# One step of a hybrid decoder: gating stage in another order, unit matrix first, residual loads in SyncE's queue

## What is computed

```python
# layer 0, part B: chunked gating
vn = layer_norm(v, ln_g, ln_b)
ws = tril(w_s)                                   # 8 groups of 128x128
mixed = einsum('gij,bcjgd->bcigd', ws, vp) + b_s # vp: vn in chunks
out_b = u * mixed * silu(gate)
# layer 0, sample group: 8 queries over 256 cached keys (2 pages each) and their own
p = softmax(logits + alibi + mask); o = p @ v_sel
x1 = LayerNorm(ALPHA * x + concat(out_a, out_b) @ e_w_out)
# layer 1: recurrence over time, per head, with S of 64x64
S = S * w_t + sa * (kk_t * a_t) + v_t * k_t;  out_t = S @ r_t
y = LayerNorm(ALPHA * x1 + gated(out) @ c_w_out)
```

## Time and profile before

| | us |
|---|---|
| median of 3 runs | 2238.67 (2236.12 to 2243.87) |
| profiled execution | 2245.97 |
| its span, first to last instruction | 2244.2 |
| PE busy | 1830.0 (82%) |
| DVE busy | 1239.5 (55%) |
| ACT busy | 575.7 |
| POOL busy | 402.2 |
| gating stage | 879 to 1113 |
| recurrence | 1806 to 2048 |
| last projection | 2051 to 2244 |

### The profile page before, as it was taken

How to read it: one execution, slowest core, us unless ns; L and a number is a source line. 1 busy time by engine, 2 the same in 40 slices (tenths; PEclk the granted TensorE clock), 3 DMA queues, 4 the chain that set the end, 5 groups by cost and what they waited for, 6 DMA issues and landing times. The chain is left out here.

```text
span 2244.2 us, 30621 instructions
## 1 busy us (share of the span) xinstructions
PE 1830.0 (82%) x11638; PEld 1063.9 (47%) x11638; DVE 1239.5 (55%) x2382; ACT 575.7 (26%) x1153; POOL 402.2 (18%) x376
## 2 busy tenths in 40 slices
PE   8999467899984996599747999978989947772877
PEld 4445134444433774365233666644455436662432
DVE  2000074888897763654466667677533326562485
ACT  0000015400013552111045545561122014340100
POOL 0001110000023552110000233320013312232110
PEclk9999688999996998689876999988988979995999
DMA  4100724222111003621164344534847395755510
GB/s 176 71 33 34 208 73 129 80 75 72 75 39 67 29 20 116 220 99 44 59 129 170 104 140 139 146 116 101 146 124 137 95 218 140 183 135 162 171 67 38
DMA packets 277601, 245.65 MB, mean 109 GB/s; under 512 B 131997, under 2 KB 229309, under 8 KB 277197
## 3 DMA queue, kind: packets, MB, share of 16 engines
q1 hardware_dynamic: 271988, 227.36, 35.7%
q0 software_dynamic: 2976, 9.02, 1.1%
q10 hardware_dynamic: 2496, 7.37, 1.1%
HBM read 161.60 MB, written 86.63 MB: 111 GB/s over the span
## 5 line engine op out<-in xcount | busy, mean ns | idle before, releaser
L1761 PE MATMUL ri_ps<-ri_xm,ri_w 128*128 128x384 f32 (+1 forms) x768 | 233.1, 458 | 0.1
L555 PE MATMUL ix_ps<-ix_src,ei_xT 128*128 128x512 f32 x512 | 223.5, 599 | 9.3 <-DMA ix_src<-in_e_w_in 9.3
L1857 PE MATMUL ri_ps<-ri_w,ri_xm 128*128 128x512 f32 x512 | 227.3, 607 | 0.0
L186 PE MATMUL ei_ps<-ei_w,ei_xT 128*128 128x512 f32 (+1 forms) x432 | 188.4, 598 | 3.9 <-DMA ei_w<-in_e_w_in 3.9
L1761 PEld LDWEIGHTS ri_ps<-ri_xm,ri_w 128*128 128x128 f32 x768 | 145.2, 191 | 73.8 <-issue 2.6
L633 DVE TENSOR_SCALAR_CACHE_REDUCE ix_flags<-score,ix_cand 128x384 bf16<-128x384 f32 (+1 forms) x186 | 163.7, 943 | 12.2 <-DVE ix_cand L650 12.0
L555 PEld LDWEIGHTS ix_ps<-ix_src,ei_xT 128*128 128x128 f32 x512 | 98.0, 192 | 132.3 <-issue 122.8
L1857 PEld LDWEIGHTS ri_ps<-ri_w,ri_xm 128*128 128x128 f32 x512 | 99.6, 195 | 124.8 <-issue 124.7
L1348 PE MATMUL co_psm<-co_w,co_srcT 128*128 128x512 f32 (+1 forms) x288 | 128.6, 606 | 15.2 <-DVE co_y L1403 14.4
L186 PEld LDWEIGHTS ei_ps<-ei_w,ei_xT 128*128 128x128 f32 (+1 forms) x432 | 77.6, 181 | 113.8 <-issue 113.8
L1106 PE MATMUL go_psm<-go_w,go_srcT 128*128 128x512 f32 (+1 forms) x288 | 129.7, 610 | 0.0
(11 more groups left out here) (328 smaller groups left out, 3021.6 us busy)
## 6 DMA issues: line engine op xcount, KB each, us to landing
ix_src<-in_e_w_in SPq DMA_DIRECT2D x4, 2048.0 KB, 11.1
scratch_h<-ix_stage SPq DMA_DIRECT2D x32, 256.0 KB
ri_w<-in_c_w_in SPq DMA_DIRECT2D x16, 512.0 KB, 5.6
ri_w<-in_c_w_in SPq DMA_DIRECT2D x4, 2048.0 KB, 8.6
ei_w<-in_e_w_in SPq DMA_DIRECT2D x3, 2048.0 KB, 19.6
scratch_h<-ei_stage POOLq DMA_DIRECT2D x24, 256.0 KB, 2.3
ix_src<-scratch_h SPq DMA_DIRECT2D x3, 2048.0 KB, 8.4
go_uvg<-scratch_h SPq DMA_DIRECT2D x8, 768.0 KB, 6.6
```

What stands on the lines that cost most here:

```text
L186: last = nc.tensor.matmul(ps[n % NB][0:rows(t), 0:cw], xT[:, kd, t * P:t * P + rows(t)], rhs, start=(kd == 0), stop=(kd == KD - 1))
L555: last = nc.tensor.matmul(ps[n % NB][:], xT[:, kd, t * P:(t + 1) * P], w_rest[s % 2][:, kd], start=(kd == 0), stop=(kd == KD - 1))
L1761: last = nc.tensor.matmul(out[:, 0:wd], w[:, ct % 2, kd, i * P:(i + 1) * P], xm[:, i, kd, lo:lo + wd], start=(kd == 0), stop=(kd == KD - 1))
L1857: last = nc.tensor.matmul(out[:], xm[:, j, kd, t * P:(t + 1) * P], w[:, a, kd], start=(kd == 0), stop=(kd == KD - 1))
```

## The change

1. Gating stage, SyncE: `upper` is issued ahead of uvg(0); w(0) goes ahead of src(0) and uvg(1); uvg(2) and src(1) go ahead of the sample's loads; the loads of `w00` and `b00` go to the end of the prologue and get a semaphore of their own, waited for only by the last tile's gate. The 16 page loads are issued in four parts, in steps 1 to 4, behind load_uvg.
2. Gating stage, TensorE: a step is project(s-2), mixed(s), transposes(s-1). `turn` is in step 5, and the value products come in steps 6 and 7, four samples in each.
3. Gating stage, ScalarE and VectorE: the y activation (L1154) stands ahead of the srcT copies. The sample's softmax stands behind `finish`, its first half in step 2, its second in step 3, `shares` in step 4 and `own_value` in step 5.
4. Recurrence: the two loads of `eye` go first in the queue.
5. Last projection: all residual, gain and offset loads leave ScalarE's queue for SyncE's. res(0), gain and offset stand behind src(2), the sample step's whole part 0 (`side.sync(sp, 0)`) behind them, then src(3), res(1), src(4), res(2) and so on.

```diff
-    def pages(self, sp):
-        sp.wait_ge(self.pt_in, 16)
+    def pages(self, sp, part):
+        if part == 0:
+            sp.wait_ge(self.pt_in, 16)
...
-        for b in range(DB):
+        for b in (2 * part, 2 * part + 1):
...
@@ phase_gate_out, SyncE
+            sp.dma_start(upper[:], g["c_uppereq"]).then_inc(c_in, 16)
             load_uvg(0)
-            sp.dma_start(upper[:], g["c_uppereq"]).then_inc(c_in, 16)
             sp.dma_start(bgam[:], ...).then_inc(c_in, 16)
             sp.dma_start(bbet[:], ...).then_inc(c_in, 16)
             sp.dma_start(bs[:], ...).then_inc(c_in, 16)
+            load_w(0)
             load_src(0)
             load_uvg(1)
-            load_w(0)
             load_w(1)
-            sp.dma_start(w00[:], ...).then_inc(c_in, 16)
-            sp.dma_start(b00[:], ...).then_inc(c_in, 16)
+            load_uvg(2)
+            load_src(1)
             side.loads(sp)
-            load_src(1)
             load_res(0)
...
-            load_uvg(2)
             load_src(2)
             load_res(1)
-            side.pages(sp)
             load_res(2)
+            sp.dma_start(w00[:], ...).then_inc(own_in, 16)
+            sp.dma_start(b00[:], ...).then_inc(own_in, 16)
             for s in range(1, NT + 4):
                 if s + 2 <= LAST:
                     load_uvg(s + 2)
+                if s <= 4:
+                    side.pages(sp, s - 1)
@@ phase_gate_out, TensorE
             for s in range(NT + 3):
+                if s >= 2:
+                    project(s - 2)
                 if s < NT:
                     mixed(s)
-                if s == 3:
+                if s == 5:
                     side.turn(pe)
-                if 4 <= s < 4 + DB // 2:
-                    side.values(pe, 2 * (s - 4))
+                if s in (6, 7):
+                    side.values(pe, 4 * (s - 6))
...
                     transposes(s - 1)
-                if s >= 2:
-                    project(s - 2)
@@ phase_gate_out, VectorE
-            dve.wait_ge(c_in, 16 * 6)
+            dve.wait_ge(c_in, 16 * 4)
...
                     gate(s - 1)
-                if s == 1:
-                    side.logits(dve)
-                if s == 2:
-                    side.shares(dve)
-                if s == 4:
-                    side.own_value(dve)
...
                 if s >= 3:
                     finish(s - 3)
+                if s in (2, 3):
+                    side.logits(dve, s - 2)
+                if s == 4:
+                    side.shares(dve)
+                if s == 5:
+                    side.own_value(dve)
@@ phase_out, SyncE
             for t in tiles:
+                if t == 3:
+                    side.sync(sp, 0)
                 if t not in side.late:
                     load_src(sp, t)
...
+                else:
+                    load_res(t - 2)
+                if t == 2:
+                    sp.dma_start(gam[:], gain_d.partition_broadcast(P)).then_inc(g_in, 16)
+                    sp.dma_start(bet[:], bias_d.partition_broadcast(P)).then_inc(g_in, 16)
+            for t in (NT - 1, NT):
+                load_res(t)
@@ phase_wkv, SyncE
+            for h in range(2):
+                sp.dma_start(eye[half(h)], g["c_ident"][half(h), half(h)]).then_inc(c_in, 16)
             load_bk(0)
             load_ra(0)
             sp.dma_start(mb[:], g["c_mb"]).then_inc(c_in, 16)
-            for h in range(2):
-                sp.dma_start(eye[half(h)], g["c_ident"][half(h), half(h)]).then_inc(c_in, 16)
```

More of the change, by code:

```diff
@@ L886, in scalar, with logits @@
         self.nc.scalar.activation(self.lrow[:], self.lrow[:], ACT.Exp).then_inc(self.exped, 1)
-    def logits(self, dve):
+    def logits(self, dve, part):
         nc, lrow, mx = self.nc, self.lrow, self.mx
-        self.link = link = Chain(dve, self.link_v)
-        dve.wait_ge(self.own_in, 16 * 3)
-        link(nc.vector.tensor_tensor(lrow[:], lrow[:], self.alibi[:], ALU.add))
-        link(nc.vector.tensor_tensor(lrow[:], lrow[:], self.score_s[0:DB, 0:SKEYS].unsqueeze(1).broadcast_to([DB, H, SKEYS]), ALU.add))
+        if part == 0:
+            self.link = Chain(dve, self.link_v)
+        link = self.link
+        if part == 0:
+            dve.wait_ge(self.own_in, 16 * 3)
+            link(nc.vector.tensor_tensor(lrow[:], lrow[:], self.alibi[:], ALU.add))
+            link(nc.vector.tensor_tensor(lrow[:], lrow[:], self.score_s[0:DB, 0:SKEYS].unsqueeze(1).broadcast_to([DB, H, SKEYS]), ALU.add))
+            return
         link(nc.vector.tensor_reduce(mx[:], lrow[:], AX.X, ALU.max))
@@ L935, in values @@
         pe.wait_ge(self.cache_in, 16 * 2 * DB)
-        for b in range(b0, b0 + 2):
+        for b in range(b0, b0 + DB // 2):
             for ct in range(4):
@@ L984, in phase_gate_out @@
         uvg_in, src_in, res_in = ([sem(f"{n}{i}") for i in range(RING)] for n in ("uvg_in", "src_in", "res_in"))
-        ws_tr, wsT_d, half_d = sem("ws_tr"), sem("wsT_d"), sem("half_d")
+        ws_tr, wsT_d, half_d, own_in = sem("ws_tr"), sem("wsT_d"), sem("half_d"), sem("own_in")
         boff_d, bnorm_d, off_d, norm_d = sem("boff_d"), sem("bnorm_d"), sem("off_d"), sem("norm_d")
@@ L1043, in _ @@
             sp.dma_start(bet[:], g["ln_b"][0].partition_broadcast(P)).then_inc(g_in, 16)
-            load_uvg(2)
             load_src(2)
             load_res(1)
-            side.pages(sp)
             load_res(2)
+            sp.dma_start(w00[:], g["b_ws"][:, 0, 0:1].rearrange("g o -> (g o)").partition_broadcast(DB), **small).then_inc(own_in, 16)
+            sp.dma_start(b00[:], g["b_bs"][:, 0:1].rearrange("g o -> (g o)").partition_broadcast(DB), **small).then_inc(own_in, 16)
             for s in range(1, NT + 4):
@@ L1138, in _ @@
                     nc.scalar.activation(vn[0:m, k], slot(uvg, s)[:, AW:2 * AW], ACT.Identity, scale=brs[0:m, k:k + 1], bias=boff[0:m, k:k + 1]).then_inc(bnorm_d, 1)
-                if s == 2:
+                if s >= 3:
+                    t = s - 3
+                    m, k = rows(t), t % 2
+                    act.wait_ge(off_d, t + 1)
+                    nc.scalar.activation(y[0:m, k], y[0:m, k], ACT.Identity, scale=rstd[0:m, k:k + 1], bias=off[0:m, k:k + 1]).then_inc(norm_d, 1)
+                if s == 4:
                     side.scalar(act)
@@ L1149, in _ @@
                                        ps_t[half][:].rearrange("p (j n) -> p j n", j=4)[:, :, 0:m]).then_inc(srcT_d, 1)
-                if s >= 3:
-                    t = s - 3
-                    m, k = rows(t), t % 2
-                    act.wait_ge(off_d, t + 1)
-                    nc.scalar.activation(y[0:m, k], y[0:m, k], ACT.Identity, scale=rstd[0:m, k:k + 1], bias=off[0:m, k:k + 1]).then_inc(norm_d, 1)
         @block.gpsimd
@@ L1204, in gate @@
                     dve.wait_ge(vn_d, t + 1)
+                    dve.wait_ge(own_in, 32)
                     link(nc.vector.tensor_tensor(hd(o), hd(vn[0:m, k]), w00[:].unsqueeze(2).broadcast_to([DB, H, HD]), ALU.mult))
@@ L1294, in _, with load_res @@
         def _(sp):
+            def load_res(t):
+                sp.dma_start(res[0:rows(t), t], residual_of(t)).then_inc(res_in[t], 16)
             sp.dma_start(ident[:], ident_d).then_inc(c_in, 16)
             for t in tiles:
+                if t == 3:
+                    side.sync(sp, 0)
                 if t not in side.late:
                     load_src(sp, t)
-                if t == 0:
-                    side.loads(sp)
                 if t < 2:
@@ L1353, in _ @@
         def _(act):
-            for t in tiles:
-                act.dma_start(res[0:rows(t), t], residual_of(t)).then_inc(res_in[t], 16)
-                if t == 1:
-                    act.dma_start(gam[:], gain_d.partition_broadcast(P)).then_inc(g_in, 16)
-                    act.dma_start(bet[:], bias_d.partition_broadcast(P)).then_inc(g_in, 16)
             for n in range(2 * (NT + 1)):
```

9 lines of the change are left out of this document (4 added, 5 removed).

## The result

| | before | after |
|---|---|---|
| median of 4 runs, us | 2241.27 (2236.12 to 2248.51) | 2211.15 (2206.20 to 2214.73) |
| profiled execution, span | 2244.2 | 2211.4 |
| mean granted TensorE clock | 0.889 | 0.897 |

The ratio is 0.9864, 95% interval 0.9844 to 0.9884: 30 us faster. 2207 was forecast, 2193 to 2222 the range.

A forecast was written before the change was run, and what follows sets the result against it. No one engine bounds the kernel; five stages follow each other with barriers, three touched. Gains of 16.7 (28.8 less 12.1), 1.9 and 13 sum to 31.6 us, off the 2238.67 median: 2207 us, range 2193 to 2222.

The forecast's parts named there:

- Gating start: Gating stage: first projection starts 28.8 us earlier, bounds 22 to 32.
- Gating steps: Gating stage: TensorE has 12.1 us more work and waiting behind its earlier start.
- (1): Gating stage: mixed(2) and transposes(1) now come after project(0) instead of before it, +2.7 us.
- (2): Gating stage: each projection waits for ScalarE's copies of its own transposes, 0.88 us at 8 tiles, +7.0 us.
- (3): Gating stage: value products in two runs of 64 records instead of four of 32, +2.4 us, bounds -10 to +8.
- Rival A: Gating stage: the clock falls in each step, about +14 us, time 2221; chance 0.10.
- Recurrence: Recurrence's start: with the unit matrix first, the first product comes 1.9 us earlier, bounds nothing and 3.
- Last projection: Last projection: the sample's step(1) starts earlier and the rest shifts with it, 13 us gained, bounds 6 to 20.
- Rival B: Last projection: SyncE's queue is the wall, sample's vectors come no earlier, stage gains nothing, time 2220; chance 0.11.
- D: Gating start: another first-step input comes at 904, so the stage gains 2.6 us, time 2221; chance 0.05.
- C: Gating stage: clock stays low through projections, 27.5 us instead of 13.9; one in two slow, +54, time 2261; chance 0.04.

The follow-up runs named there:

- start_only: Kernel before, with only the gating stage's new prologue load order and own semaphore for w00 and b00; 2228.18 us, ratio 0.9938.
- gate_only: Kernel before, with the whole changed gating stage, recurrence and last projection as before; 2227.88 us, ratio 0.9947.
- side_late: Changed kernel, with the sample step's loads back behind all the last projection's loads in SyncE's queue; 2220.74 us, ratio to before 0.9912.
- values_between: Changed kernel, with two value products behind each matmul of projections 4 and 5 instead of two separate runs; 2193.85 us, ratio to before 0.9804.
- eye_only: Kernel before, with only the unit matrix's loads put first in the recurrence's queue; 2242.78 us, ratio 1.0020.
- no_eye: Changed kernel, with the recurrence's unit matrix loads back behind mb; 2209.74 us, ratio to before 0.9877.
- all3_no_eye: Changed kernel with half-tile waits, value products between projection matmuls, parameter loads from ScalarE, and the unit matrix back behind mb; 2187.91 us, ratio to before 0.9770.
- par_act: Changed kernel, with the sample step's 32 small parameter loads issued from ScalarE's queue in tile 1; 2209.44 us, ratio to before 0.9870.
- split_wait: Changed kernel, where a projection first waits for half its transposed tile, and for the rest at its fifth contraction block; 2199.69 us, ratio to before 0.9826.

## Why the prediction was right, and where it was not

**Gating start, 28.8 us forecast: right.** 59.3 to 30.3 is 29.0. The mask is released by bs, at 9.6 us after the first load (889, less 879.1, was forecast: 9.9), and the next wait is for uvg(1), as forecast. start_only shows that the new order of loads and the own semaphore give 11.4 us of the early start. The other 17.6 come from the moved softmax and from TensorE's new order together, and no run parts the two. In start_only project(0) still stands behind mixed(2), which waits for gate(1), and starts 5.1 us after mixed(2) does. In the changed kernel gate(1) is over at 914.65, so with TensorE's old order project(0) would have started near 919.8 and not at 911.22: by this estimate TensorE's order is worth some 8.6 of the 17.6.

**Gating steps, 12.1 us forecast, 14.7 measured: right in kind, a little small.** (1) and (2), moved work and holes, came as said: the distance from transposes to projection grew from 0.93 to 1.77, 0.84 a tile where 0.88 was forecast. (3), the value runs, 11.79 and 10.11 where 11.8 was forecast; with the slow projections behind them +2.6 where +2.4 was. What was missing from the sum, though within the bounds, is the first projection's low clock: 16.90 against 14.25, +2.65. It is not a fixed cost: 14.00 to 17.06 in ten profiles of this order, 15.7 on average, so 1.5 belonged in the sum and the rest in the range. Rival A named the mechanism that the experiments then found to be the expensive one. It does not act in each step: projections 1 to 3 and 7 took 14.00 in all ten profiles. It acts behind the value runs, in most of the first projections, and at times behind the sample's small transposes (`turn`): there project(4) took 15.70 in gate_only and side_late and 14.00 in five others. A value run costs 14.1 us with what follows it, instead of the 7.15 of values_between. That the value products could be had so cheaply was not considered; the sum took the run as the only form.

**Recurrence, 1.9 us forecast: wrong.** The profile pair shows 2.1 us, and would have confirmed it. The step that failed is that mb, now last of the three loads of c_in, still lands 6.1 us after its issue. That time belonged to mb's old place. In all six profiles of the old order mb landed in 6.1 to 6.3 us, and the second half of the unit matrix, last of the three, in 6.7 to 10.0. In the eight of the new order the unit matrix landed in 1.9 to 2.1, and mb, last of the three, in 7.2 to 11.3. And the last of the three is issued at nearly the same time in both orders, 3.2 to 3.6 us after the stage's first load (1806.18 before, 1790.54 after), behind the same four blocks B, K, R and A. The first row is from before, its second issue at 1809.66; the other is from the changed kernel:

```profile
1809.06 1.18 SPq L2285 DMA_DIRECT2D wk_eye<-c_ident  x2
...
1794.04 0.50 SPq L2298 DMA_DIRECT2D wk_mb<-c_mb  x1
```

The order changed the name of the releaser, from wk_eye to wk_mb, and gained no time: the wait is on average 1.7 longer with the new order, within a scatter of some 4, and eye_only, no_eye and all3_no_eye find no gain (eye_only 1.0020, interval from 1.0004). The forecast's lower bound, nothing, is what came. Why mb takes longer in that place than the unit matrix did is open. Even in the pair, where the start was 2.1 us earlier, the stage was not shorter: 244.7 and 244.9.

**Last projection, 13 us forecast, 17.3 measured: mechanism right, size off.** The step that failed is that each of SyncE's issues would take 2.1 us, half a megabyte at 249 GB/s. Four weight loads took 2.81 together, src(2) 3.17, the next three about 1.1 each: S came 14.4 us after the first load where 21 was forecast. Against it, S to step(1) took 30.7 us, where 28.3 was taken and 31.2 had been measured before; taking the old row would have been better than working the chain down. The working counted 20.5 us of bare issues and 2.5 of landing, and left out the landing of the vectors' own write behind S, which par_act shows at 22.1 us with no issue behind it. -6.4 and +2.4 make the 4 us. src(1) landed 16.7 after the start, not 14. The queue moved 215 GB/s there and not 249, which for the 3.2 MB makes 2 of the 2.7 us:

```profile
2035.00:2050.00 15.00, 7.47 (x48) 5.14 (x48) 5.90 (x5) 1.17 (x2) 0.20 (x2) 0.72 0.90 215
```

This was worth nothing, as side_late shows: an earlier project(0) is not what counts. Rival B was the right place to look, and fell: it is SyncE's queue that sets the end, in both kernels, and the place of the sample's loads in it decides. What side_late does not tell is how much of the 17.3 the new place would have given with the residual loads left in ScalarE's queue; that was not tried.

**The Trainium skill**, "DMA: Bandwidth & Descriptors", section Issuing engines are not separate DMA queues, says that issuing from several engines saves issue time and no more. The runs agree: 5.3 MB moved to the other queue lengthened nothing, and par_act, which issues 32 small loads from ScalarE, gained 3.2 us. What the traces add is what the sharing cost here. In the kernel before, ScalarE's queue moved 4.75 of 7.34 MB, which no engine waited for yet, while TensorE idled 16.45 us for src(1).

```profile
DMA packets 2605, 7.34 MB, mean 282 GB/s; under 512 B 216, under 2 KB 344, under 8 KB 2604
...
q10 hardware_dynamic: 1295, 4.75, 58.8%
q1 hardware_dynamic: 1309, 2.58, 33.9%
```

That is 2050.0 to 2076.0, before; q10 is ScalarE's, q1 SyncE's. In the changed kernel, 2035.0 to 2060.0:

```profile
DMA packets 2648, 5.51 MB, mean 220 GB/s; under 512 B 173, under 2 KB 301, under 8 KB 2646
...
q1 hardware_dynamic: 2646, 5.48, 96.6%
```

**The total.** Forecast -31.6; the profiled pair -32.8, the medians -30.1. That they lie so close is in part luck: 4.3 too little in the last stage, and 2.4 and 2.1 too much in the other two, cancel, and 1.4 of the pair's difference lies in stages of the same code. D, the forecast of a late second input, did not come; C neither.

## What to carry to other kernels

Ask of each stage which one step sets its end, and put that step's loads first in its queue: 14.5 us of earlier TensorE work gained 1.8, while 17.3 us of earlier sample vectors gained 17.3. Put thin matmuls between thick ones rather than in a run of their own, and let a matmul wait only for the half of its input that it reads first; by the ratios to the kernel before, that was 13 to 15 and 9 to 10 us below the changed kernel here, though split_wait's interval touches the changed kernel's and only 5.3 of its gain are the wait's own. A landing time belongs to a place in the queue, not to a tile: where several loads share a semaphore, ask when the last of them is issued and how long the last one took before, in several executions.

## What the runs showed of the hardware

- 32 products of 128x2 (64 records) cost 7.15 us when spread between the 16 matmuls of a projection, at a granted clock of 1.00. In one run they cost 9.6 to 11.8 us, at 0.50 from 2 to 4.6 us on, and the projection behind them took 14.58 to 16.71 instead of 14.00.
- The same first projection, behind the same 4 us wait, mixed and transposes, took 14.00 in gate_only and 16.90 in the changed kernel, whose code is the same up to there: the granted clock was 1.00 in its first 4 us in the one and 0.50 in the other. In all ten profiles of this order the time goes with the clock of the first 14 us, from 1.00 at 14.00 us to 0.78 at 17.06. What decides the clock is open.
- Four issues of 0.5 MB each took SyncE 15.66 us while ScalarE's queue was loaded too, and 2.81 with its own alone, at the same place in the kernel. A second queue is not the only thing that holds an issue: in the changed gating stage, with SyncE's queue alone, that of src(0) took 3.71.
- In the last stage's start the two queues together moved 282 GB/s, the one 220. One queue can move more: 362 GB/s in the changed gating stage, 905 to 919.
- The 32 parameter loads took ScalarE's queue 3.74 to 3.93 us per eight. In SyncE's, behind S, two groups of eight took 3.66 and the other two 6.20 and 7.00.
